# Sixteen 32x32 tiles in place of two full-width products: the weighted sums of a gathered expert layer

## The chip, the cores and the metric

The kernel runs on one core of a Trainium2 chip. The metric is the device time of one execution in microseconds. The kernel before took 2930.46 us (median of three runs, 2928.35 to 2935.43). The engines are called as in the profile: PE is TensorE, PEld its weight loads, DVE VectorE, ACT ScalarE, POOL GpSimd, SP SyncE.

## The reference

Everything is float32. The first block has two layers of attention followed by a retrieval layer (PEER), and a second block (retention, gated delta net, routed experts) follows. The change touches the retrieval alone. For each chunk of 128 tokens it is

```python
u_sel = jnp.take(u, eidx, axis=0)
a = jax.nn.gelu(jnp.einsum('chkd,cd->chk', u_sel, xc), approximate=False)
w = (g * a).astype(x.dtype)
v_sel = jnp.take(v, eidx, axis=0)
return jnp.einsum('chk,chkd->cd', w, v_sel)
```

with 8 heads h and 16 experts k for each token c, so 128 selected rows for each token, and D = 1024. There are 256 tokens, so two chunks, in each of two layers. The last line, the weighted sum of the gathered v rows, is what is changed.

## The kernel before

**The loop.** In each layer, `n` runs from 0 to 255: `c = n // 128` is the chunk, `n % 128` the selected row of each of the 128 tokens. Token p lies on partition p. For each n:

- POOL issues `gather(n)` (L2419), an indirect DMA that brings u and v of one expert for each token side by side, 128 rows of 2048 floats, into `landing(n)`, one of `GATHERS = 8` places. It first waits until the weighted sum n-8 has used the place (`("used", "gather", l, n - 8)`).
- DVE runs `dots(n)` (L1341): the dot product of the u half with the token's h.
- ACT runs `weigh(n)`: Gelu, times the softmax weight, and then `diagonals[n % 2]`, the identity scaled by the weight of each partition (L125, 128x128). It waits for the weighted sum n-2 first, since there are two diagonals.
- PE runs `weighted_sum(n)` (L155 is its helper): the diagonal is the stationary operand, the v half the moving one, two products of 512 columns into two banks of PSUM, accumulated over 128 n.

**Beside it.** Each engine carries other work in its own fixed program order between these steps: `route(q + 1)` on DVE (the top-k of the next quarter of the rows, in 24 pieces at n % 64 = 2, 4, ... 48), and a `background` generator on all engines which advances one step at the n that `beside(l, n)` names: every sixth n in layer 0, every third in layer 1 (the second block's context work). POOL advances its background five n behind its gathers, so a background step of POOL which waits for DVE holds back the gathers behind it.

**The ends of the chunks.** When the sum of a chunk is complete, `finish(c)` on DVE adds it to `ALPHA * h` from PSUM (L89, two instructions of 128x512), and a layer norm follows. `finish(0)` starts on DVE after `dots(130)` (`NORM_AT[0] = 130`), and its steps are spread over the n up to 138. `finish(1)` stands after the loop, and the next stage waits for it. Chunk 0 accumulates in banks 0 and 1, chunk 1 in banks 2 and 3 (`SUMS`); the background has banks 4 to 7 (`OTHERS`). `fresh` makes PE wait until a bank's old content was read. Vector instructions in a chain wait each for the one before.

Of the kernel before, what the change touches and what calls it, by code (L numbers as in the profile page):

```python
# [5 lines left out]
P = 128  # L6
ALU = mybir.AluOpType
# [183 lines left out]


GATHERS = 8
SUMS, OTHERS = ((0, 1), (2, 3)), (4, 5, 6, 7)
WQ_AT = (4, 8, 16, 0)
UNITS = [(0, 0), (0, 1), (1, 0), (1, 1)]
ROUTE_PIECES, EXP_AT, WEIGHTS_AT = 24, 50, 54
# [101 lines left out]
def build(nc, d, out):  # L299
    import numpy as np  # L300
    ctx = ExitStack()
    with ctx:
# [53 lines left out]
        def ar(o, n):  # L356
            assert o + n <= ARENA
            return arena[:, o:o + n]
# [30 lines left out]
        norm_scratch = ar(2048, 1024)  # L389
        SC = ar(0, 4096)  # L390
        gs, aa = ar(9056, 256), ar(9312, 256)
        diagonals = [ar(8800, 128), ar(8928, 128)]
        mod_rows = ar(20480, 2048)
        silu_cols = ar(19840, 256).rearrange("p (k s) -> p k s", k=8)

# [22 lines left out]
        def tensor_program(pe):  # L418
# [178 lines left out]
            def peer(l, background):  # L597
                qT = ar(14720, 4096).rearrange("p (m t) -> p m t", m=16)
                keys = R(12, 2)
                s = 2 * l + 1  # L600

                def turned_rows(c):
                    pe.wait_ge(*at("h", s, c))
                    for k0 in (0, 4):
                        b = fresh("hT", s, c, k0)
                        turn4(b, lambda k: h[:, c, k * P:(k + 1) * P], k0, "hT", s, c, k0)

                def queries(i, c):
                    b = fresh("q", l, i, c)
                    pe.wait_ge(*at("loaded", "wq", l, i))  # L610
                    for k0 in (0, 4):
                        pe.wait_ge(*at("out", "hT", s, c, k0))
                    for m in range(4):
                        for k in range(8):
                            t = pe.mm(b[:, m * P:(m + 1) * P], R(WQ_AT[i], 4)[:, k * 512 + m * P:k * 512 + (m + 1) * P],
                                      hT[:, k, c * P:(c + 1) * P], k == 0, k == 7)
                    pe.done(t, ("ps", "q", l, i, c))
                    if c == 1:
                        pe.tell(("used", "wq", l, i))

                def scores(c, hf):
                    for j in (2 * hf, 2 * hf + 1):
                        b = fresh("s", l, c, j)
                        pe.wait_ge(*at("loaded", "keys", l))
                        pe.wait_ge(*at("out", "q", l, j, c))
                        for m in range(4):
                            hp = 4 * j + m
                            t = pe.mm(b[:, m * P:(m + 1) * P], qT[:, hp, c * P:(c + 1) * P], keys[:, hp * P:(hp + 1) * P])
                        pe.done(t, ("ps", "s", l, c, j))
                    pe.tell(("used", "keys", l))  # L630

                def weighted_sum(n, two):

                    c, k = n // 128, n % 128
                    pe.wait_ge(*at("diagonal", l, n))
                    for x in range(2):
                        t = pe.mm(two[x][:, :], diagonals[n % 2], landing(n)[:, D + 512 * x:D + 512 * x + 512],
                                  k == 0, k == 127)
                    pe.done(t, ("used", "gather", l, n))
                    if k == 127:  # L640
                        pe.tell(("ps", "acc", l, c, 0), ("ps", "acc", l, c, 1))

                for hf in range(2):
                    for c in range(2):
                        if hf == 0 and c == 0:
                            turned_rows(0)
                        queries(2 * hf, c)
                        queries(2 * hf + 1, c)
                        if hf == 0 and c == 0:
                            turned_rows(1)  # L650
                        scores(c, hf)
                for n in range(256):
                    if n % 128 == 0:
                        two = [fresh("acc", l, n // 128, x, among=SUMS[n // 128]) for x in range(2)]
                    weighted_sum(n, two)
                    advance(background, beside(l, n))
                for _ in background:
                    pass
# [407 lines left out]
        def vector_program(v):  # L1066
# [220 lines left out]
            def peer(l, background):  # L1287
# [55 lines left out]
                        accum_out=aa[:, n:n + 1]), ("dots", l, n))  # L1343

                def finish(c):
                    for i in range(2):
                        x = h[:, c, i * 512:(i + 1) * 512]
                        v.wait_ge(*at("ps", "acc", l, c, i))
                        v.stt(x, x, ALPHA, tile_of("acc", l, c, i)[:, :], ALU.mult, ALU.add, ("out", "acc", l, c, i))
                    yield from layer_norm_parts(2 * l + 2, (c,), R(14, 1), R(15, 1), (("ln2", l, 0), ("ln2", l, 1)))  # L1350
                    yield

# [589 lines left out]
        def scalar_program(a):  # L1942
# [110 lines left out]
            def peer(l, background):  # L2053
# [21 lines left out]
                def weigh(n):  # L2075
# [5 lines left out]
                    a.act(w, w, ACT.Copy, scale=gs[:, n:n + 1])  # L2081
                    if n > 1:
                        a.wait_ge(*at("used", "gather", l, n - 2))
                    a.act(diagonals[n % 2], ident, ACT.Copy, ("diagonal", l, n), scale=w)

                for hf in range(2):
                    for c in range(2):
# [685 lines left out]
def constants():  # L2773
# [3 lines left out]
    t = {}  # L2777
# [33 lines left out]
            rows[n * x:n * x + n, j] = T * (j % 2)  # L2811
    t["slot_rows"] = rows
    t["rel"] = i[None, :] - i[:, None]
    t["fold"] = i[:, None] % 32 == np.arange(2)[None, :]
    at, o = {}, 0
    for k, v in t.items():
# [82 lines left out]
```

## Time and profile before

| | |
|---|---|
| time, median of three runs | 2930.46 us |
| time of the profiled execution | 2929.8 us |
| its span | 2928.0 us |
| granted TensorE clock over the span | 0.92 |
| gather loop of layer 0, from first to last landing | about 260 to 936 us |
| gather loop of layer 1 | about 1158 to 1830 us |
| TensorE records | 9692 weight loads, 9692 matmuls |

A float32 product stands in the trace as two weight loads and two matmul records, so a weighted sum before is four matmul records. Busy times are sums over records of an engine; the DMA share is the mean busy share of the core's 16 DMA engines.

### The profile page before, as it was taken

To read this page: it belongs to the slowest core of one execution; us is meant where nothing else is said; L and a number is where in the kernel's file an instruction comes from. 1 tells how busy PE (TensorE), PEld (TensorE's weight loads), DVE (VectorE), ACT (ScalarE), POOL (GpSimd) and SP (SyncE) were. 2 spreads that over 40 slices of the span, in tenths; PEclk is the share of its full clock that TensorE was granted. 3 is DMA by queue.
4 is the path that set the end of the run, shared out by engine and by line. 5 is a ranking of instruction groups with operands and counts; after the bars stand their busy time and mean duration, and the time that the engine had idled before them with its cause. 6 is when DMAs were issued, how large, how long until landed. Compare 5 with 4: busy or idle time off the path is not lost.

```text
span 2928.0 us, 29445 instructions
## 1 busy us (share of the span) xinstructions
PE 2373.3 (81%) x9692; PEld 1312.7 (45%) x9692; DVE 1583.3 (54%) x3250; ACT 840.9 (29%) x2292; POOL 849.7 (29%) x723
## 2 busy tenths in 40 slices
PE   6989798888887989798888998889878787667673
PEld 3657333343422559353444443568764532222221
DVE  4426857678545545888989765455552522121111
ACT  1412443434433311343443533322210111111110
POOL 1002443435432111455455553012110111222221
PEclk9999999999999889999999999899989778888887
DMA  7744999999999414999999999412112599999994
GB/s 281 278 153 191 421 422 418 416 422 389 418 423 372 169 55 162 378 421 375 410 382 406 407 422 406 158 44 73 58 62 101 213 404 401 388 390 382 382 380 142
DMA packets 130130, 891.18 MB, mean 304 GB/s; under 512 B 23216, under 2 KB 23600, under 8 KB 31792
## 3 DMA queue, kind: packets, MB, share of 16 engines
q0 software_dynamic: 86976, 553.74, 47.0%
q1 hardware_dynamic: 42992, 335.46, 28.6%
q8 instruction: 79, 1.29, 0.2%
q14 instruction: 83, 0.68, 0.1%
HBM read 880.18 MB, written 40.37 MB: 314 GB/s over the span
## 4 chain that ended last, share of the span: by engine, by line
PE 42%; DMA 26%; DVE 23%; ACT 4%; issue 3%; SPq 1%; POOL 1%; DVEq 0%; ACTq 0%; POOLq 0%
PE ps L155 40%; DMA ring<-in_peer_uv,idx_u 11%; DVE ring L1341 7%; DMA ring<-in_w_gu 6%; DVE arena L76 5%; DMA ring<-in_w_down 3%; ACT arena L125 3%; PE ps L158 2%; DMA arena<-in_peer_uv,idx_u 1%; DVE arena L109 1%; DVE iu L113 1%; DVE arena L1341 1%; SPq L2601 1%; DMA arena<-in_w_gu 1%; DMA arena<-in_w_down 1%
## 5 line engine op out<-in xcount | busy, mean ns | idle before, releaser
L155 PE MATMUL ps<-ring,arena 128*128 128x512 f32 (+3 forms) x3456 | 1292.9, 650 | 297.6 <-ACT arena L125 171.5
L155 PEld LDWEIGHTS ps<-ring,arena 128*128 128x128 f32 (+2 forms) x3456 | 476.6, 176 | 983.4 <-issue 599.0
L1341 DVE CUSTOM_DVE_ANT_0 ring<-ring,h 128x1024 f32<-128x1024 f32 x448 | 560.2, 1250 | 291.8 <-DMA ring<-in_peer_uv,idx_u 255.7
L2419 POOL DMA_INDIRECT ring<-in_peer_uv,idx_u x448 | 506.3, 1130 | 684.7 <-PE ps L155 540.9
L155 PE MATMUL ps<-arena 128*128 128x128 f32 (+7 forms) x2504 | 489.9, 377 | 92.7 <-ACT arena L125 34.3
L125 ACT ACTIVATE arena<-arena 128x1 f32<-128x1 f32 (+3 forms) x1093 | 294.2, 269 | 741.0 <-DVE arena L1341 632.8
L155 PEld LDWEIGHTS ps<-arena 128*128 128x128 f32 (+3 forms) x2504 | 309.8, 190 | 257.7 <-issue 147.7
L76 DVE TENSOR_TENSOR arena<-arena,ps 128x512 f32<-128x512 f32 (+1 forms) x158 | 93.7, 593 | 433.4 <-ACT arena L125 359.6
L125 ACT ACTIVATE arena<-ps 128x512 f32<-128x512 f32 (+5 forms) x192 | 106.4, 554 | 757.0 <-PE ps L155 708.8
L155 PE MATMUL ps<-ring,hT 128*128 128x512 f32 (+2 forms) x896 | 311.3, 509 | 15.4 <-DVE hT L97 9.9
L125 ACT ACTIVATE arena<-cst,arena 128x128 f32<-128x128 f32 x512 | 205.5, 401 | 127.4 <-PE ps L155 86.5
L155 PEld LDWEIGHTS ps<-ring,hT 128*128 128x128 f32 x896 | 174.2, 201 | 141.6 <-issue 115.9
L2556 POOL DMA_INDIRECT y_tab<-arena,iu x64 | 100.1, 1565 | 435.5 <-DVE arena L97 309.0
L134 POOL TENSOR_TENSOR small<-small,cst 128x1 f32<-128x1 f32 (+3 forms) x42 | 46.8, 1114 | 562.2 <-DVE small L84 548.1
L155 PE MATMUL ps<-hT,ring 128*128 128x128 f32 (+1 forms) x1280 | 180.5, 304 | 12.0 <-ACT hT L125 12.0
L155 PEld LDWEIGHTS ps<-hT,ring 128*128 128x128 f32 x1280 | 169.8, 198 | 20.6 <-issue 10.5
L158 PE MATMUL ps<-cst,arena 128*128 128x128 f32 (+1 forms) x706 | 115.3, 313 | 57.6 <-DVE arena L76 30.0
L158 PEld LDWEIGHTS ps<-cst,arena 128*128 128x128 f32 (+1 forms) x706 | 93.8, 158 | 114.5 <-issue 45.5
L97 DVE COPY arena<-ps 128x512 f32<-128x512 f32 (+5 forms) x102 | 59.6, 584 | 150.3 <-PE ps L155 81.7
L134 POOL TENSOR_TENSOR arena<-arena,cst 128x512 f32<-128x512 f32 (+2 forms) x52 | 68.9, 1325 | 217.2 <-DVE arena L76 118.5
L1341 DVE CUSTOM_DVE_ANT_0 arena<-arena,h 128x1024 f32<-128x1024 f32 x64 | 82.1, 1283 | 40.6 <-DMA arena<-in_peer_uv,idx_u 35.0
L2419 POOL DMA_INDIRECT arena<-in_peer_uv,idx_u x64 | 72.8, 1138 | 102.7 <-PE ps L155 100.0
(116 smaller groups left out, 1383.5 us busy)
## 6 DMA issues: line engine op xcount, KB each, us to landing
ring<-in_w_gu SPq DMA_DIRECT2D x98, 1024.0 KB, 28.8
ring<-in_w_down SPq DMA_DIRECT2D x52, 1024.0 KB, 29.4
ring<-in_w_in SPq DMA_DIRECT2D x16, 2048.0 KB, 12.4
arena<-in_w_gu SPq DMA_DIRECT2D x30, 1024.0 KB, 29.6
ring<-in_w_mod SPq DMA_DIRECT2D x12, 2048.0 KB, 8.0
ring<-in_peer_wq SPq DMA_DIRECT2D x8, 2048.0 KB, 8.3
ring<-in_w_o SPq DMA_DIRECT2D x6, 2048.0 KB, 15.2
ring<-in_w_gates SPq DMA_DIRECT2D x12, 1024.0 KB, 4.9
```

Of the source, the lines that this page charges most:

```text
L76: self.done(self.e.tensor_tensor(o, a, b, op), *names)
L97: self.done(self.e.tensor_copy(o, a), *names)
L109: self.done(self.e.max(out=o, in_=a), *names)
L113: self.done(self.e.max_index(o, m, a), *names)
L125: self.done(self.e.activation(o, a, f, **k), *names)
L134: self.done(self.e.tensor_tensor(o, a, b, op), *names)
L155: return self.e.matmul(o, lhsT, rhs, start=start, stop=stop, skip_group_check=True)
L158: return self.e.transpose(o, src, ident)
L1341: v.done(v.e.tensor_tensor_reduce(out=row, in0=row, in1=h[:, n // 128, :], scale=1.0, scalar=0.0, op0=ALU.mult, op1=ALU.add, accum_out=aa[ ...
L2419: g.e.indirect_dma_start(out=landing(n), out_offset=None, in_=d["peer_uv"], in_offset=bass.IndirectOffsetOnAxis(ap=idx_u[:, n:n + 1], axis ...
L2556: g.e.indirect_dma_start(out=y_tab, out_offset=index(m.add_to, n), in_=m.yb[s % 2], in_offset=None, bounds_check=2 * T - 1, oob_is_err=Fal ...
L2601: sp.e.dma_start(o, src).then_inc(sem, 16)
```

## The change

Each weighted sum is done as sixteen products instead of two. D is cut in four quarters x of 256 columns. For each quarter, the 128 tokens are cut in four groups r of 32, and group r of quarter x is computed on its own 32x32 tile of the array: rows 32r to 32r+31, columns of group r XOR x. So quarter x has its own bank, and in it the token groups stand permuted by r XOR x. The stationary operand is a 32-column diagonal (`ident4` repeats a 32x32 identity for each group of 32 partitions). All four banks 0 to 3 are used by both chunks. `finish` now reads quarter 0 in one instruction and the others in four each, which undo the permutation.

```diff
-SUMS, OTHERS = ((0, 1), (2, 3)), (4, 5, 6, 7)
+SUMS, OTHERS = (0, 1, 2, 3), (4, 5, 6, 7)
...
-        diagonals = [ar(8800, 128), ar(8928, 128)]
+        diagonals = [ar(8800, 32), ar(8928, 32)]
...
-                    for x in range(2):
-                        t = pe.mm(two[x][:, :], diagonals[n % 2], landing(n)[:, D + 512 * x:D + 512 * x + 512],
-                                  k == 0, k == 127)
+                    for x in range(4):
+                        for r in range(4):
+                            i, o = slice(32 * r, 32 * r + 32), slice(32 * (r ^ x), 32 * (r ^ x) + 32)
+                            t = pe.mm(four[x][o, 0:256], diagonals[n % 2][i, :], landing(n)[i, D + 256 * x:D + 256 * x + 256],
+                                      k == 0, k == 127)
...
-                        two = [fresh("acc", l, n // 128, x, among=SUMS[n // 128]) for x in range(2)]
-                    weighted_sum(n, two)
+                        four = [fresh("acc", l, n // 128, x, among=SUMS) for x in range(4)]
+                    weighted_sum(n, four)
...
-                    for i in range(2):
-                        x = h[:, c, i * 512:(i + 1) * 512]
-                        v.wait_ge(*at("ps", "acc", l, c, i))
-                        v.stt(x, x, ALPHA, tile_of("acc", l, c, i)[:, :], ALU.mult, ALU.add, ("out", "acc", l, c, i))
+                    v.wait_ge(*at("ps", "acc", l, c, 0))
+                    for q in range(4):
+                        for r in range(1 if q == 0 else 4):
+                            i, o = (slice(0, P),) * 2 if q == 0 else (slice(32 * r, 32 * r + 32),
+                                                                      slice(32 * (r ^ q), 32 * (r ^ q) + 32))
+                            x = h[i, c, 256 * q:256 * q + 256]
+                            v.stt(x, x, ALPHA, tile_of("acc", l, c, q)[o, 0:256], ALU.mult, ALU.add,
+                                  ("out", "acc", l, c, q))
...
-                    a.act(diagonals[n % 2], ident, ACT.Copy, ("diagonal", l, n), scale=w)
+                    a.act(diagonals[n % 2], C("ident4"), ACT.Copy, ("diagonal", l, n), scale=w)
...
+    t["ident4"] = i[:, None] % 32 == np.arange(32)[None, :]
```

## Rows read from the trace of the kernel before

**Rows 1.** The page: busy times of the engines, and GB/s in 40 slices.

```profile
PE 2373.3 (81%) x9692; PEld 1312.7 (45%) x9692; DVE 1583.3 (54%) x3250; ACT 840.9 (29%) x2292; POOL 849.7 (29%) x723
...
GB/s 281 278 153 191 421 422 418 416 422 389 418 423 372 169 55 162 378 421 375 410 382 406 407 422 406 158 44 73 58 62 101 213 404 401 388 390 382 382 380 142
```

**Rows 2.** Busy time by stretch: window, length, engines, granted clock, DMA share, GB/s.

```profile
278.00:936.00 658.00, 547.48 (x1269) 231.18 (x1267) 439.88 (x906) 260.29 (x803) 276.26 (x251) 0.96 1.00 415
640.00:665.00 25.00, 18.07 (x37) 7.29 (x37) 22.71 (x58) 9.31 (x31) 11.59 (x9) 0.93 0.97 388
1172.00:1829.60 657.60, 567.00 (x1802) 278.67 (x1801) 526.53 (x1013) 273.99 (x835) 325.94 (x272) 0.97 0.98 401
1190.00:1215.00 25.00, 18.34 (x45) 8.62 (x46) 21.88 (x62) 11.58 (x31) 5.74 (x6) 0.80 0.99 411
1215.00:1240.00 25.00, 20.32 (x66) 9.74 (x64) 22.95 (x49) 8.27 (x27) 14.31 (x13) 1.00 0.80 304
1370.00:1395.00 25.00, 19.61 (x67) 9.85 (x66) 22.99 (x47) 7.78 (x25) 16.13 (x12) 1.00 0.83 328
1525.00:1550.00 25.00, 19.69 (x63) 9.84 (x64) 22.77 (x61) 8.45 (x28) 16.01 (x13) 0.93 0.83 330
1700.00:1800.00 100.00, 89.73 (x291) 43.32 (x290) 64.44 (x98) 38.95 (x125) 47.78 (x43) 1.00 1.01 421
```

**Rows 3.** The longest wait of DVE from 1190 to 1284 us: total, times, longest.

```profile
DVE ring L1341 <- DMA ring<-in_peer_uv,idx_u: 0.6, 1, 0.6
```

**Rows 4.** Timeline of POOL: start, length, instruction, idle before it, releaser.

```profile
1217.68 0.94 POOL L2419 DMA_INDIRECT ring<-in_peer_uv,idx_u  x1 [0.44 <-PE ps L155]
1223.05 3.46 POOL L134 TENSOR_TENSOR arena<-arena,cst 128x512 f32<-128x512 f32 x2 [4.43 <-DVE arena L76]
1226.66 0.96 POOL L2419 DMA_INDIRECT ring<-in_peer_uv,idx_u  x1
...
1511.00 0.94 POOL L2419 DMA_INDIRECT ring<-in_peer_uv,idx_u  x1 [7.21 <-PE ps L155]
```

**Rows 5.** Timeline of the end of layer 1's gather loop, all engines.

```profile
1827.19 1.23 DVE L1341 CUSTOM_DVE_ANT_0 ring<-ring,h 128x1024 f32<-128x1024 f32 x1 [1.26 <-DMA ring<-in_peer_uv,idx_u]
...
1829.65 1.23 DVE L1341 CUSTOM_DVE_ANT_0 ring<-ring,h 128x1024 f32<-128x1024 f32 x1 [1.22 <-DMA ring<-in_peer_uv,idx_u]
...
1831.54 0.40 ACT L125 ACTIVATE arena<-cst,arena 128x128 f32<-128x128 f32 x1
1831.99 0.30 PEld L155 LDWEIGHTS ps<-ring,arena 128*128 128x128 f32 x2 [1.30 <-ACT arena L125]
1831.99 1.98 PE L155 MATMUL ps<-ring,arena 128*128 128x512 f32 x4 [0.47 <-ACT arena L125]
...
1834.02 1.41 DVE L89 SCALAR_TENSOR_TENSOR h<-h,ps 128x512 f32<-128x512 f32 x2 [3.13 <-PE ps L155]
```

**Rows 6.** Timeline of DVE: finish(0) of layer 1, and eight chained instructions of 256 columns.

```profile
1508.33 1.41 DVE L89 SCALAR_TENSOR_TENSOR h<-h,ps 128x512 f32<-128x512 f32 x2
```

```profile
23.60 3.65 DVE L89 SCALAR_TENSOR_TENSOR arena<-cst 128x256 f32<-128x256 f32 x8
```

**Rows 7.** Timeline of PE: four column tiles of 32, 512 columns moving.

```profile
125.44 1.92 PE L155 MATMUL ps<-ring,arena 128*32 128x512 f32 x16
```

**Rows 8.** Timeline of PE and of its weight loads: a burst on column tiles of 32.

```profile
2358.38 1.10 PE L155 MATMUL ps<-arena 128*32 128x2 f32 x64 [2.87 <-DVE arena L76]
```

```profile
2358.38 1.01 PEld L155 LDWEIGHTS ps<-arena 128*32 128x32 f32 x64 [3.77 <-DVE arena L76]
```

**Rows 9.** Timeline of PE: an unbroken stream of full-width loads and matmuls.

```profile
1132.80 14.46 PE L155 MATMUL ps<-hT,ring 128*128 128x128 f32 x128
```

**Rows 10.** The page: instruction DMA queue, packets, MB, share of 16 engines.

```profile
q8 instruction: 79, 1.29, 0.2%
```

More of the change, by code:

```diff
@@ L630, in scores, with weighted_sum @@
                     pe.tell(("used", "keys", l))
-                def weighted_sum(n, two):
+                def weighted_sum(n, four):
                     c, k = n // 128, n % 128
                     pe.wait_ge(*at("diagonal", l, n))
-                    for x in range(2):
-                        t = pe.mm(two[x][:, :], diagonals[n % 2], landing(n)[:, D + 512 * x:D + 512 * x + 512],
-                                  k == 0, k == 127)
+                    for x in range(4):
[3 more added lines that the diff above has]
+                                      k == 0, k == 127)
                     pe.done(t, ("used", "gather", l, n))
                     if k == 127:
-                        pe.tell(("ps", "acc", l, c, 0), ("ps", "acc", l, c, 1))
+                        pe.tell(*(("ps", "acc", l, c, x) for x in range(4)))
                 for hf in range(2):
```

## The prediction

> **What bounds the kernel now.** I read the page first. It names PE as the busiest engine, 81% of the span, and shows DMA at about 421 GB/s in a long early and a long middle stretch [rows 1]. These are the two gather loops, and together they are 1.35 ms of 2.93. So the first question is whether PE or DMA sets their pace. The timeline at the end of layer 1 answers it for a quiet stretch: two dots start 2.46 us apart, each after a wait for its landing, and the sum's four matmul records take 1.98 us [rows 5]. A gather is 1 MB (128 rows of 8 KB), and at 421 GB/s that is 2.49 us. So one n costs DMA 2.49 us and PE 1.98 us and the share of the background. DMA sets the pace there; PE, at 90% busy, runs close behind [rows 2].
>
> The windows tell where DMA falls short of 421 GB/s, and this is all that a faster PE could win inside the loops. Layer 0 moved 415 GB/s over 658 us: 658 x 6/421 = 9 us lost. Layer 1 moved 401 over 657.6 us: 657.6 x 20/421 = 31 us lost [rows 2]. Together 40 us.
>
> Then I looked for what holds the gathers back in layer 1. Three windows of 25 us have 304, 328 and 330 GB/s, and lose 6.9, 5.5 and 5.4 us, 18 of the 31 [rows 2]. The timeline of POOL shows the reason for the first: after the gather at 1217.68, POOL waits 4.43 us for DVE, runs two background instructions of 3.46 us together, and only then issues the next gather at 1226.66 [rows 4]. Which engine is DVE waiting for in turn? For none: from 1190 to 1284 us its longest wait is 0.6 us [rows 3], and its busy time is 22 to 23 of 25 us [rows 2], the rest being the short gaps between chained instructions. So where layer 1 loses most, DVE is the bound, through its route pieces and background, and POOL's place behind it turns this into late gathers. PE is busy 18 to 20 of 25 us there and does not decide.
>
> **The change part by part.** I make the sum against the profiled execution (2929.8 us; the median of the runs is 0.7 us higher).
>
> *The sum itself on PE.* Two products of 512 columns become sixteen of 256 on tiles of 32x32. The trace has no tile that is cut in rows as well. The nearest row is four column tiles side by side: 16 records of 512 columns in 1.92 us, 0.12 us for each, while full-width records of the same length take about 0.5 us (1.98 for four) [rows 5, 7]. So four column tiles run at once. If row groups run at once as well, 32 records of 256 columns need a quarter of 1.71, so 0.43 us. The other limit is how fast PE gets its instructions: 32 loads and 32 matmuls for each n. A burst of 64 loads and 64 matmuls on 32-column tiles took 1.10 us, 8.6 ns for each record [rows 8], so 64 records take 0.55 us. The slowest feed I can find in an unbroken stream is 128 loads and 128 matmuls in 14.46 us, 56 ns for each record [rows 9], which is array time and an upper bound. I take the burst, whose shape is nearer: 0.55 us and a start of some 0.2, 0.75 us for a single sum. With PE less busy its granted clock may well fall from the 0.96 of these loops towards half (the window with PE busy 18 of 25 us already shows 0.80 [rows 2]), so between 0.75 and 1.2 us; I take 1.0 us against 1.98.
>
> The Trainium skill has a rule against such small products: in "TensorE: Matmul & The Clock Gate", section "Wait — 56ns, not 53.3ns?", the sequencer needs about 62 ns for each matmul when hardware decode is off. By it, as an estimate, 32 matmuls would need 1.98 us, and the change would win nothing on PE. The burst of 64 in 1.10 us speaks against it.
>
> *Term A, the ends of the two loops.* After the last landing the path is dots, weight, diagonal, sum, finish(1) [rows 5]. The sum gives back 1.98 - 1.0 = 1.0 us, and the diagonal of 32 columns instead of 128 (0.40 us before) about 0.1. finish(1) goes from two instructions in 1.41 us to thirteen of 256 columns. DVE's chained pitch for 256 columns is 3.65/8 = 0.456 us [rows 6], whatever the number of partitions that I assume; thirteen take 5.93 us, so 4.5 us more. Net 3.4 us for each layer: +6.8. Bounds 5 and 8.
>
> *Term B, finish(0) in the middle.* The same 4.5 us come to DVE after dots(130). In layer 1 it stands at 1508, DVE is as full behind it as in the stretch of [rows 3] (22.77 of 25 us), and a POOL block like that of [rows 4] follows in the 330 GB/s window [rows 2]. So all of it arrives at the gathers: +4.5. In layer 0 finish(0) stands near 610, and the window from 640 to 665 has DVE busy 22.71 of 25 us at 388 GB/s [rows 2]; it is the one short window there, DVE is freer around it, and a part falls in gaps: I take +2, between 0 and 4.5. Together +6.5, bounds 0 and 9. Since both chunks now share the banks, PE's sum 128 waits for finish(0), and behind it wait PE's later sums and background, ACT's diagonal 130, and gather 136 on POOL. In layer 1, finish(0) would end at 1508.33 + 5.93 = 1514.3, and gather 136 was issued at 1511.00 [rows 4, 6]; so it slips by some 4 to 5 us. Seven gathers of 2.49 us, 17 us of DMA work, are outstanding then and cover it. I put nothing for this wait.
>
> *Term C, instructions.* For each n PE gets 64 records instead of 8: 512 x 56 = 28,672 more. The instruction queue q8 moved 1.29 MB in 79 packets, and 1.29 MB over PE's 19,384 records is 67 bytes for each, so I read q8 as PE's queue, with 256 records in a packet of 16 KB [rows 1, 10]. That makes 1.9 MB or 117 packets more, through the same 16 engines that bound the loops. 0.2% of 16 x 2928 us is 94 us of engine time, 1.19 us for each packet. Spread evenly, 117 x 1.19/16 = 8.7 us, and in about four fifths of the loops' time DMA is the bound: +7. If they never met a saturated engine it is 0; if the worst engine gets twice the mean, 17; if all fell to one engine, 139. "Runtime: NRT & Kernel Launch" of the Trainium skill, section "Instruction fetch mechanics", says that instructions come in blocks of 16 KiB or 256 and that the fetch is hidden. The block size agrees with [rows 10]. By that rule term C is 0 and the forecast about 2940.
>
> *Term D, places free earlier.* The sum releases its place about 1 us earlier, and PE's queue of sums behind background steps gets shorter. Of the 40 us of lost DMA time, 18 stand behind POOL's waits for DVE and stay. Of the other 22 many are gathers limited by DVE in the same saturated stretches, so I take 4 us, a microsecond for each of a few late gathers: -4, bounds 0 and -22.
>
> Sum: 2929.8 + 6.8 + 6.5 + 7 - 4 = 2946.1 us, with the 0.7 us to the median 2947. The bounds give 2929.8 + 5 - 22 = 2913 and 2929.8 + 8 + 9 + 17 = 2964, without the single-engine case. The new constant adds 32 columns to a load at the start, and I cost it at nothing.
>
> **The rivals.**
> - *The release of places decides after all.* POOL's gathers often wait for PE: 7.21 us before the one at 1511.00 [rows 4]. If a faster PE removed all 40 us and the slack swallowed finish(0), the time would be 2930 - 40 + 6.8 + 7 = 2904. It decides if gathers come early enough that POOL's blocks no longer empty the queue. Against it: DVE has no waits there [rows 3]. 0.08.
> - *Same.* finish(0) falls in gaps and the packets are hidden: 2930.5 + 6.8 - 4 = 2933. 0.20.
> - *Row groups do not run at once.* Then four columns at a time as in [rows 7], about 1.7 us and the start as before; gains of A and D vanish: 2947 + 2 + 4 = 2953. 0.08. By the Trainium skill's rule on the sequencer, as an estimate, it would come to about the same.
> - *PE starves for instructions.* At 56 ns a record one n takes 3.6 us, 1.1 more than DMA's 2.49, over 512 n +570: about 3520. It decides from 39 ns a record (2.49/64). 0.04.
> - *Instruction packets pile up on one engine*: 132 us over the forecast, 3079. 0.04.
> - The forecast itself: 0.56, its own range 2936 to 2960.
>
> **How the numbers follow.** I take 0.3%, 9 us, as what a measurement can tell from no change. Faster (under 2922): the first rival and a little of term D, 0.10. Same: the second rival and the low edge of the forecast, 0.25. Slower: 0.65. The range reaches from the second rival with its spread, 2929, to the third with its own, 2968. It leaves out the first, fourth and fifth, 0.16.
>
> **What would show it.** On the page: about 57,000 to 58,000 instructions, q8 near 196 packets, PE's busy share well down and its granted clock in the loops below 0.96. In the timeline at the end of the loops: 32 matmul records of 32x256 within 0.5 to 1.2 us, and finish as thirteen instructions over 5.9 us. In layer 1's windows: DVE as busy as before, DMA still short by POOL's wait for DVE, and the third block 4 to 5 us later within the loop than before. In quiet windows such as 1700 to 1800 us: slightly under 421 GB/s. The prediction is wrong if the windows of 304 to 330 GB/s fill up (then D was the main term), if quiet windows lose more than 1.5% (then C), or if dots come further apart than 2.5 us in quiet stretches with PE as releaser.

## The result, and the profile after

The changed kernel takes 2953.24 us (median of four runs, 2951.98 to 2956.14), the kernel before 2930.26 beside it: ratio 1.0083, 95% interval 1.0069 to 1.0096. It is 23 us slower, where 17 slower was forecast. The profiled execution has a span of 2952.0 us against 2928.0.

The page of the changed kernel, to be read beside [rows 1, 10]:

```profile
span 2952.0 us, 58166 instructions
...
PE 2043.1 (69%) x24028; PEld 1172.3 (40%) x24028; DVE 1595.3 (54%) x3294; ACT 799.6 (27%) x2292; POOL 848.5 (29%) x723
...
PEclk9888577565755889686767775799998788888787
...
q8 instruction: 190, 3.11, 0.4%
```

PE has 14,336 more loads and as many more matmuls, and is 330 us less busy. Its granted clock is down to 0.5 to 0.8 in the loops, and queue q8 moves 111 packets of 16 KB more.

The windows of the changed kernel, beside [rows 2]; the window from 1240 to 1265 us is new, because the first block has moved there:

```profile
278.00:936.00 658.00, 372.85 (x8196) 141.37 (x8188) 438.67 (x908) 236.65 (x789) 276.46 (x253) 0.61 1.00 413
...
1172.00:1829.60 657.60, 414.18 (x8748) 237.69 (x8746) 522.48 (x1022) 252.88 (x824) 329.03 (x275) 0.72 0.98 401
1215.00:1240.00 25.00, 12.17 (x298) 5.16 (x296) 22.61 (x53) 11.33 (x32) 8.09 (x8) 0.70 0.96 398
1240.00:1265.00 25.00, 14.71 (x292) 8.47 (x292) 22.85 (x59) 8.00 (x29) 13.94 (x12) 0.70 0.85 339
1370.00:1395.00 25.00, 11.51 (x252) 5.11 (x268) 22.85 (x55) 10.55 (x33) 8.88 (x7) 0.51 0.75 304
1525.00:1550.00 25.00, 11.01 (x236) 5.38 (x236) 22.83 (x50) 5.01 (x16) 8.73 (x8) 0.57 0.68 259
1700.00:1800.00 100.00, 68.91 (x1443) 42.22 (x1440) 61.98 (x95) 35.73 (x125) 49.22 (x45) 0.76 1.01 419
```

PE's busy time in layer 1 fell from 567 to 414 us, and the same window still moves 401 GB/s. The three short windows are still there (339, 304, 259), with DVE at 22.8 of 25 us in each, while PE is busy half of the time. In the quiet window the rate is 419 instead of 421.

The end of layer 1's loop in the changed kernel, beside [rows 5], and finish(0) of both layers on DVE, beside [rows 6]:

```profile
1848.38 1.23 DVE L1343 CUSTOM_DVE_ANT_0 ring<-ring,h 128x1024 f32<-128x1024 f32 x1 [1.22 <-DMA ring<-in_peer_uv,idx_u]
...
1850.85 1.23 DVE L1343 CUSTOM_DVE_ANT_0 ring<-ring,h 128x1024 f32<-128x1024 f32 x1 [1.24 <-DMA ring<-in_peer_uv,idx_u]
...
1852.74 0.32 ACT L125 ACTIVATE arena<-cst,arena 128x32 f32<-128x32 f32 x1
1853.12 0.29 PEld L155 LDWEIGHTS ps<-ring,arena 32*32 32x32 f32 x32 [2.18 <-ACT arena L125]
1853.12 1.17 PE L155 MATMUL ps<-ring,arena 32*32 32x256 f32 x32 [1.30 <-ACT arena L125]
1854.46 5.84 DVE L89 SCALAR_TENSOR_TENSOR h<-h,ps 128x256 f32<-128x256 f32 x13 [2.37 <-PE ps L155]
```

```profile
617.61 5.84 DVE L89 SCALAR_TENSOR_TENSOR h<-h,ps 128x256 f32<-128x256 f32 x13
...
1525.29 5.84 DVE L89 SCALAR_TENSOR_TENSOR h<-h,ps 128x256 f32<-128x256 f32 x13
```

The dots still come 2.47 us apart, each after its landing. The sum takes 1.17 us instead of 1.98, and finish 5.84 us instead of 1.41.

The start times of the dots, n = 0, 128, 136 and 255 of each layer, divide every trace in the same way. The table has one profiled execution of each kernel; the last three rows are of the experiments with chunk 0's norm moved to n = 200. All in us.

| kernel | before loop 0 | loop 0 | in it n 128 to 136 | between | loop 1 | in it n 128 to 136 | rest | span |
|---|---|---|---|---|---|---|---|---|
| before | 260.3 | 676.1 | 22.4 | 221.3 | 671.9 | 27.6 | 1098.3 | 2928.0 |
| changed | 265.1 | 685.4 | 26.8 | 223.4 | 676.9 | 31.7 | 1101.1 | 2952.0 |
| e1_finish13 | 265.5 | 680.8 | 26.8 | 225.6 | 673.5 | 31.7 | 1102.2 | 2947.6 |
| e2_unpermuted | 262.1 | 682.1 | 22.4 | 220.9 | 674.0 | 27.8 | 1099.0 | 2938.2 |
| e3_zeros14 | 266.5 | 810.8 | 33.5 | 227.6 | 833.7 | 27.1 | 1106.3 | 3244.9 |
| e4_tiles64 | 262.7 | 674.9 | 23.1 | 219.1 | 666.9 | 27.9 | 1097.6 | 2921.2 |
| e5_before_lag8 | 260.5 | 680.4 | 22.4 | 218.3 | 666.7 | 26.7 | 1095.5 | 2921.4 |
| e6_before_lag3 | 265.3 | 687.0 | 22.4 | 223.1 | 685.5 | 27.6 | 1098.4 | 2959.3 |
| e7_tiles64_lag8 | 258.5 | 673.0 | 23.1 | 217.9 | 669.9 | 27.0 | 1095.3 | 2914.6 |
| e8_after_lag8 | 265.4 | 681.1 | 26.8 | 223.9 | 676.8 | 30.8 | 1100.7 | 2947.9 |
| e12_sp_waits | 258.2 | 676.5 | 22.4 | 221.1 | 691.6 | 27.6 | 1636.6 | 3483.9 |
| e9_before_norm200 | 260.6 | 674.5 | 19.9 | 220.4 | 664.4 | 23.3 | 1101.7 | 2921.6 |
| e10_finish13_norm200 | 258.3 | 674.9 | 19.9 | 224.2 | 662.0 | 23.3 | 1103.7 | 2923.0 |
| e11_tiles64_norm200 | 264.8 | 673.4 | 20.7 | 218.1 | 660.8 | 23.5 | 1100.9 | 2917.9 |

The changed kernel's 24.0 us of span are 4.8 before the first loop, 9.3 and 5.0 in the loops (4.4 and 4.1 of these between n = 128 and 136), 2.1 between the layers and 2.8 after. Single traces differ in code that no version changes: the first column reaches from 258.2 to 266.5, and the profiled execution of a kernel lies up to 10 us from the kernel's median (e6 2961.15 against 2951.32, e7 2916.41 against 2924.88). So a difference of one column between two traces is certain only to several us. The column n 128 to 136 is firmer: in layer 0 it is 22.4 in all five traces that have the old finish at n = 130 and PE's full-width or (r, r) sums, and 26.8 in all three with thirteen instructions there; in layer 1 it is 26.7 to 27.8 and 30.8 to 31.7.

### The profile page after: what moved, and what is told of

Same layout as the page of the kernel before. It is cut to its first block, busy times and chain, and to the rows that moved or that the text cites. A ratio compares the mean times of both kernels' runs of the same rounds, so it can differ in the third digit from the quotient of the medians.

```text
span 2952.0 us, 58166 instructions
## 1 busy us (share of the span) xinstructions
PE 2043.1 (69%) x24028; PEld 1172.3 (40%) x24028; DVE 1595.3 (54%) x3294; ACT 799.6 (27%) x2292; POOL 848.5 (29%) x723
## 4 chain that ended last, share of the span: by engine, by line
PE 36%; DMA 31%; DVE 24%; issue 3%; ACT 3%; SPq 1%; POOL 1%; DVEq 0%; another core or an unknown queue 0%; ACTq 0%; POOLq 0%
PE ps L155 34%; DMA ring<-in_peer_uv,idx_u 18%; DVE ring L1343 8%; DMA ring<-in_w_gu 7%; DVE arena L76 5%; DMA ring<-in_w_down 3%; ACT arena L125 2%; PE ps L158 2%; DVE arena L109 1%; DVE iu L113 1%; DVE arena L1343 1%; SPq L2607 1%; DMA arena<-in_w_gu 1%; DVE h L89 1%; DVE arena L97 1%
## 5 line engine op out<-in xcount | busy, mean ns | idle before, releaser
L155 PE MATMUL ps<-ring,arena 32*32 32x256 f32 (+4 forms) x16000 | 926.4, 556 | 580.5 <-ACT arena L125 431.4
L155 PEld LDWEIGHTS ps<-ring,arena 32*32 32x32 f32 (+3 forms) x16000 | 302.0, 127 | 1087.9 <-ACT arena L125 685.6
L155 PE MATMUL ps<-arena 32*32 32x256 f32 (+8 forms) x4296 | 490.6, 456 | 152.2 <-ACT arena L125 82.3
L155 PEld LDWEIGHTS ps<-arena 32*32 32x32 f32 (+4 forms) x4296 | 327.9, 174 | 299.7 <-ACT arena L125 136.7
L125 ACT ACTIVATE arena<-cst,arena 128x32 f32<-128x32 f32 x512 | 164.5, 321 | 112.1 <-PE ps L155 59.8
```

The costliest lines, as they stand in the source:

```text
L125: self.done(self.e.activation(o, a, f, **k), *names)
L155: return self.e.matmul(o, lhsT, rhs, start=start, stop=stop, skip_group_check=True)
```

## The experiments

The kernel before took 2927.36 us beside e1 to e4 (17 runs), 2927.88 beside e5 to e8 (23) and 2927.71 beside e9 to e12 (21). Ratios are to these.

### e1_finish13: only the thirteen instructions of finish

```diff
-                    for i in range(2):
-                        x = h[:, c, i * 512:(i + 1) * 512]
-                        v.wait_ge(*at("ps", "acc", l, c, i))
-                        v.stt(x, x, ALPHA, tile_of("acc", l, c, i)[:, :], ALU.mult, ALU.add, ("out", "acc", l, c, i))
+                    v.wait_ge(*at("ps", "acc", l, c, 0))
+                    for q in range(4):
+                        for r in range(1 if q == 0 else 4):
+                            i = slice(0, P) if q == 0 else slice(32 * r, 32 * r + 32)
+                            x = h[i, c, 256 * q:256 * q + 256]
+                            v.stt(x, x, ALPHA, tile_of("acc", l, c, q // 2)[i, 256 * (q % 2):256 * (q % 2) + 256],
+                                  ALU.mult, ALU.add, ("out", "acc", l, c, q // 2))
```

> The kernel before, with only finish changed: thirteen chained instructions of 256 columns (three quarters of D in groups of 32 partitions) in place of two of 512. The sums are as before. My theory (terms A and B): 4.5 us more at both ends and at finish(0) of layer 1, 2 to 4.5 us at finish(0) of layer 0, so +15 to +18, about 2947 us. Rival, finish(0) is absorbed in DVE's gaps: only the two ends count, +9, 2939 us. If the time stays within 3 us of before, the finish is not what made the changed kernel slower.

2947.73 us (2939.43 to 2953.5), ratio 1.0066, interval 1.0047 to 1.0084: 20 us slower, most of what the change costs. Two of its six executions took 2939 us and four 2947 to 2954. The timeline of this kernel shows the four finishes as in the changed one; here is DVE at the end of layer 1:

```profile
1849.79 5.83 DVE L89 SCALAR_TENSOR_TENSOR h<-h,ps 128x256 f32<-128x256 f32 x13 [3.13 <-PE ps L155]
```

The parts stand where terms A and B put them: 4.4 and 4.1 us between n = 128 and 136 of the two layers, 4.3 between the layers and 3.9 after. Layer 0's is as large as layer 1's. Together they are 16.7 us, of the 15 to 18 that I expected; in this trace the first loop also starts 5.2 us later. The steps are not made up for later: against before, this kernel's dots are 0.1 us early at n = 128 of layer 0, 4.4 late at 132 and 4.7 at 255; in layer 1 they are 2.6 early, then 1.6 late at 132 and still 1.6 at 255. (That layer 1's whole loop is only 1.6 us longer comes from its first eight n, which took 2.0 us less.) And since this kernel has the old banks, and the changed kernel has the same two steps of 4.4 and 4.1, the sharing of the banks adds nothing to them. Behind n = 136 no run has the shared banks alone: in layer 0 the changed kernel loses another 1.2 us to n = 144, where e1 gains 1.2.

### e2_unpermuted: only the small tiles and their instructions

Sixteen products for each row as in the change, but group r always on tile (r, r), two quarters in the two halves of one bank, and finish as before. What it changes in the computation: a tile starts its sum in both halves of a bank, and the sums that come out are not quite the reference's; the instructions and their sizes are those of the change.

```diff
+                    for x in range(4):
+                        for r in range(4):
+                            i, y = slice(32 * r, 32 * r + 32), slice(256 * (x % 2), 256 * (x % 2) + 256)
+                            t = pe.mm(two[x // 2][i, y], diagonals[n % 2][i, :],
+                                      landing(n)[i, D + 256 * x:D + 256 * x + 256], k == 0, k == 127)
```

> Sixteen 32x32 products for each row as in the changed kernel, but every token group stays on its own columns (tile r, r for all quarters), so two banks for each chunk, finish and the banks' waits are as before. It has the changed kernel's instruction count without its finish. Only four of the sixteen tiles are ever in use, so the sum should take about 1.7 to 2.0 us, as before. Theory (term C): instruction packets on the DMA engines cost +5 to +9 us, 2936 to 2939 us, and quiet windows move 418 to 419 GB/s instead of 421. Rival, packets are hidden: 2930 us plus or minus 2. Rival, products on one tile do not overlap at all: 16 x 0.43 us for each row, over 4000 us.

2939.44 us (2934.33 to 2940.77), ratio 1.0041, interval 1.0028 to 1.0055. The last sum, the quiet window and the page's row of q8 of this kernel:

```profile
1841.37 1.93 PE L155 MATMUL ps<-ring,arena 32*32 32x256 f32 x32 [1.44 <-ACT arena L125]
```

```profile
1700.00:1800.00 100.00, 92.22 (x1416) 53.62 (x1408) 65.97 (x97) 34.91 (x122) 51.64 (x43) 1.00 1.01 420
```

```profile
q8 instruction: 191, 3.13, 0.4%
```

And the windows around the last sum, of the changed kernel and then of e2, for their granted clock:

```profile
1850.00:1855.00 5.00, 2.34 (x64) 0.58 (x64) 1.74 (x4) 1.32 (x5) 0.00 (x0) 0.50 0.00 2
```

```profile
1838.00:1844.00 6.00, 3.85 (x64) 1.80 (x64) 1.87 (x3) 0.82 (x3) 0.00 (x0) 1.00 0.00 0
```

Two things follow. First, 32 records on four tiles take 1.93 us at the full clock, about the 1.98 of four full-width records; on sixteen tiles the same 32 take 1.17 us at half of it (0.50, the 1.2 GHz level). Each tile works through its own records one after another (eight here, two in the change), and the start times in the traces show it: here the 32 matmul records start in eight groups of four, with about 196 ns between the groups, in the change in two groups of sixteen, with 315 ns between them. So the gain comes from all sixteen tiles being in use, which is what the permutation is for. Second, with the sum as slow as before and finish unchanged, what is left is the 112 packets and PE's 64 records for each n in place of 8: the two loops are 6.0 and 2.1 us longer, 8 together, and the timed difference is 12 us (8 to 16). Term C said 7. This run does not tell the packets from PE's work on the records; PE's busy time in the quiet window is 92.2 of 100 us instead of 89.7.

### e3_zeros14: 28 more small record pairs between the full-width ones

Fourteen products of zero (an off-diagonal 32x32 block of the diagonal, two columns) between the two full-width products of each row, added to the sum.

```diff
+                        if x:
+                            for z in range(14 if 0 < k < 127 else 0):
+                                pe.mm(two[0][32:64, 2 * z:2 * z + 2], diagonals[n % 2][0:32, 32:64],
+                                      landing(n)[0:32, D:D + 2], False, False)
```

> The kernel before with fourteen extra products of 32x32 by 2 columns for each row between its two full products (their stationary operand is the zero corner of the diagonal, so the result is unchanged): 56 more PE records for each row, as many as the changed kernel has, and nothing else. Theory (term C): +5 to +9 us from the packets, and up to 0.5 us for each row more on PE, which DMA covers in quiet stretches: 2935 to 2942 us. Rival, packets cost nothing: 2930 us. If PE's longer sum itself mattered, windows with PE as releaser of gathers would grow and the time go past 2945.

3249.21 us (3242.97 to 3250.82), ratio 1.1099, interval 1.1082 to 1.1117. The windows of layer 1 and two of its loads in the timeline of this kernel:

```profile
1172.00:1829.60 657.60, 634.28 (x6254) 418.86 (x6255) 420.23 (x931) 200.85 (x581) 221.67 (x188) 0.97 0.75 278
1700.00:1800.00 100.00, 97.34 (x1001) 58.44 (x999) 76.82 (x176) 35.00 (x106) 42.58 (x36) 0.98 0.86 316
```

```profile
1747.88 1.27 PEld L155 LDWEIGHTS ps<-ring,arena 32*32 32x32 f32 x30 [0.76 <-issue]
...
1750.77 1.27 PEld L155 LDWEIGHTS ps<-ring,arena 32*32 32x32 f32 x30 [0.76 <-issue]
```

I meant this run to add packets at no cost on PE, and it does not: 28 tiny loads on one tile, with two of the full-width ones, take 1.27 us, with a stop of 0.76 us ahead of them; the 28 start 32 ns apart. A sum with its share then takes 2.89 us (1750.77 - 1747.88), over DMA's 2.49, and PE is the bound, busy 97% of the quiet window at 316 GB/s. It says nothing on term C. What it does show is that the rival in which PE starves is real as a mechanism: 2.89 us for 64 records is 45 ns each, over the 39 from which that rival decides. It took tiny pairs on one tile beside a full-width sum; the changed kernel's 64 records in 1.17 us, spread over tiles, are 18 ns each.

### e4_tiles64: four tiles of 64x64

Four products of 512 columns on tiles of 64x64, two banks for a chunk as before, finish in three instructions.

```diff
+                        for r in range(2):
+                            i, o = slice(64 * r, 64 * r + 64), slice(64 * (r ^ x), 64 * (r ^ x) + 64)
+                            t = pe.mm(two[x][o, :], diagonals[n % 2][i, :], landing(n)[i, D + 512 * x:D + 512 * x + 512],
+                                      k == 0, k == 127)
```

> Four products on 64x64 tiles of 512 columns for each row (two halves of D, the second with the two token groups swapped), two banks for each chunk as before, finish in three instructions of 512 columns. 16 PE records for each row instead of 64, finish 0.7 us longer than before instead of 4.5. Theory: sum of about 1.0 to 1.2 us, term A about 0, term B +1, term C +1, term D -2 to -4: 2927 to 2931 us, no difference from before. Rival, a faster PE frees places and pays once its side costs are gone: 2905 to 2920 us.

2924.52 us (2918.53 to 2928.16), ratio 0.9991, interval 0.9982 to 0.9999. The last sum of its layer 0, the end of its layer 1, and its q8:

```profile
939.88 1.99 PE L155 MATMUL ps<-ring,arena 64*64 64x512 f32 x8 [0.47 <-ACT arena L125]
...
1825.91 1.09 PE L155 MATMUL ps<-ring,arena 64*64 64x512 f32 x8 [0.84 <-ACT arena L125]
1827.07 2.13 DVE L89 SCALAR_TENSOR_TENSOR h<-h,ps 128x512 f32<-128x512 f32 x3 [2.21 <-PE ps L155]
```

```profile
q8 instruction: 95, 1.56, 0.2%
```

The same idea with a quarter of the instructions has a sum of 1.09 us where the granted clock is full (1.00 from 1825.9 to 1827.0) and of 1.99 us where it is at half (0.50 from 939.9 to 941.8), which is no less than before's 1.98. It has 16 packets more, and 0.7 us more for a finish. Its loops are 1.2 and 5.0 us shorter in the traces. So the faster sum is worth at most some 6 us in the loops (term D: 4, of bounds 0 and 22), and the timed medians, 2.8 us apart in all, say rather less; it is real and small.

### e5, e6, e8 and e7: POOL's background further behind its gathers, or nearer

```diff
-                for n in range(256 + 5):
+                for n in range(256 + 8):
...
-                    if n >= 5:
-                        advance(background, beside(l, n - 5))
+                    if n >= 8:
+                        advance(background, beside(l, n - 8))
```

e6 has 3 in place of 8; e7 has this edit on e4, e8 on the changed kernel.

> Edit: the kernel before, with POOL's background eight n behind its gathers instead of five, so that a background step that waits for DVE stands behind three more gathers; all else unchanged. Theory (of the 31 us of DMA time that layer 1 loses, 18 are lost because POOL waits for DVE in three background blocks while its gathers stand behind it): three more gathers of 2.49 us are then queued ahead of each block, the windows of 304 to 330 GB/s rise towards 400, and the time falls by 5 to 12 us, ratio 0.996 to 0.998. Rival (DVE itself is full in these stretches, so the dots come no earlier whatever POOL does, or the eight places are used up anyway): the place is given free by a sum that stands behind the same dots, and nothing moves, within 2 us.

> Edit: the kernel before, with POOL's background three n behind its gathers instead of five. Theory (POOL's wait for DVE costs DMA time): the blocks hold back the gathers two n longer, layer 1's three short windows become shorter still, and the time rises by 3 to 15 us. Rival (DVE's fullness alone sets the loss): within 2 us.

> Edit: four products for each row on tiles of 64x64 (e4_tiles64: 2924.5 us, 0.9991 of before) and POOL's background eight n behind its gathers. Theory (a faster sum can give only what POOL's blocks leave it): the two gains add or more, 2912 to 2918 us, ratio 0.994 to 0.997. Rival (both touch the same lost DMA time, or none): no more than the better of the two alone, 2920 to 2925 us.

> Edit: the changed kernel, with POOL's background eight n behind its gathers instead of five. Theory (the faster sum of the changed kernel, which gave back only about 2 to 3 us, is kept from more by POOL's blocks): 5 to 15 us less than the changed kernel, 2938 to 2948 us. Rival (the places are held by dots and not by the sum): as the changed kernel, 2951 to 2955 us.

e5: 2930.1 us (2923.21 to 2939.36), ratio 1.0008, interval 0.9998 to 1.0018. e6: 2951.32 (2951.01 to 2961.15), 1.0086, 1.0071 to 1.01. e7: 2924.88 (2916.41 to 2932.8), 0.9994, 0.9985 to 1.0003. e8: 2943.5 (2942.31 to 2950.33), 1.0057, 1.0043 to 1.0071.

My theory for e5 fell. The first of layer 1's blocks, two windows of the kernel before, then the same two of e5:

```profile
1215.00:1240.00 25.00, 20.32 (x66) 9.74 (x64) 22.95 (x49) 8.27 (x27) 14.31 (x13) 1.00 0.80 304
1240.00:1265.00 25.00, 20.99 (x70) 10.80 (x71) 22.84 (x41) 9.70 (x31) 12.18 (x11) 1.00 1.01 422
```

```profile
1215.00:1240.00 25.00, 21.04 (x67) 10.00 (x65) 22.99 (x49) 7.78 (x25) 12.89 (x12) 0.98 0.96 353
1240.00:1265.00 25.00, 20.70 (x70) 10.62 (x71) 22.76 (x41) 10.20 (x32) 14.29 (x12) 1.00 0.97 373
```

This block is smoothed out and nothing is won: 304 + 422 and 353 + 373 are both 726. DVE has 23 of 25 us in all four rows, so the hole in the transfers is here only where DVE's lack of time shows. The other two blocks are less even: the second gains (328 + 423 before, 389 + 403 in e5, from 1370 to 1420 us, again with DVE near 23 of 25), the third does not (330 + 420, then 352 + 385). The trace of e5 has layer 1's loop 5.2 us shorter and layer 0's 4.3 us longer, and the median does not fall. So between 5 and 8 POOL's distance decides nothing in sum; that DVE alone decides in every block is not shown. Nearer is another matter. In e6 POOL's steps really hold the gathers back: both loops are longer, by 11 and 14 us. For the changed kernel a distance of 8 gave a ratio of 1.0057 instead of 1.0083, some 8 us (the intervals overlap at their ends). But e8's five executions fall in two groups, 2942 to 2944 and 2950 us, about as far apart as the first column's 258 and 266. The traced one is of the upper group and starts its first loop at 265.4, like the changed kernel's; against that one it gains 4 us, in layer 0's loop. More than these 4 is not shown, nor why they are won there. e7 adds nothing to e4, as e5 added nothing to before.

### e9, e10, e11: chunk 0's norm where DVE is free

```diff
-NORM_AT = (130, 131, 133, 137, 138)
+NORM_AT = (200, 201, 203, 207, 208)
```

e9 has it on the kernel before, e10 on e1, e11 on e4. From n = 192 on no route piece is left.

> Edit: the kernel before, with finish(0) and the rest of chunk 0's norm spread over n = 200 to 208 instead of 130 to 138, where no route piece stands beside them (about 6.5 us of DVE work in each layer). Theory (DVE's full stretches, not POOL's place nor PE, set the lost DMA time, and what is taken off DVE there comes back whole): layer 1's loop is 5 to 7 us shorter, layer 0's 2 to 6, the time 2917 to 2923 us. Rival (the loss has another cause, and DVE's work moves freely): within 3 us of before.

> Edit: e1 (finish in thirteen instructions, 2947.7 us) with chunk 0's norm at n = 200 to 208. Theory (term B was 4.5 us in each layer because DVE was full behind n = 130): both finish(0) are covered at n = 200, the step between n = 128 and 136 disappears and no other takes its place; against e9 only the two finish(1) remain, +9 us, 2926 to 2932 us, some 15 to 20 below e1. Rival (4.5 us on DVE's chain cost 4.5 us wherever they stand): e9 + 18 us, and a step of 4 us at n = 200 instead.

> Edit: e4 (four products on tiles of 64x64, 2924.5 us, 0.9991) with chunk 0's norm at n = 200 to 208. Theory: the two gains add, 2912 to 2920 us, the best of all. Rival (same lost DMA time, won once): as e9.

e9: 2917.11 us (2915.46 to 2923.42), ratio 0.9964, interval 0.9951 to 0.9978. e10: 2929.46 (2924.83 to 2940.25), 1.0012, 1.0001 to 1.0023. e11: 2919.84 (2917.6 to 2920.66), 0.9972, 0.9963 to 0.9982.

The windows of e9 around n = 128, beside the 330 GB/s of [rows 2]:

```profile
1500.00:1525.00 25.00, 17.87 (x43) 8.13 (x44) 22.10 (x55) 11.27 (x35) 11.69 (x9) 0.86 0.97 393
1525.00:1550.00 25.00, 22.66 (x81) 11.89 (x80) 22.56 (x60) 9.28 (x29) 16.71 (x13) 1.00 1.01 412
```

This settles what bounds the stretch behind n = 128. With some 6.5 us of DVE work taken away, the step from n = 128 to 136 is 4.3 us shorter in layer 1 and 2.5 in layer 0, the hole is filled, and layer 1's loop is 7.5 us shorter. It is 10.6 us for one line, and the lowest median of all. The edit moves POOL's step of the norm along with DVE's, so the two are not told apart here; and for the blocks at 1215 and 1370 us, where no run moved work, that DVE is the bound rests on the windows. e10 shows the same for the thirteen instructions: at n = 200 the loops are no longer than e9's (+0.4 and -2.4), so 4.4 us more on DVE cost nothing where DVE has room, and only the two finish(1) are left (3.8 between the layers and 2.0 after in the traces; 12 us in the timed medians, 9 by the rows of finish). e11 is e9 again: the gain of the small tiles, 3 us in e4, is not added. For the changed kernel I did not try it; there finish(0) cannot move to n = 200, since PE's sum 128 waits for it to empty the shared banks.

### e12_sp_waits: packets for an engine that has nothing to do

```diff
+            for n in range(255):
+                for _ in range(112):
+                    sp.e.wait_ge(*at("dots", 1, n))
```

> Edit: the kernel before, with 112 waits on an already reached semaphore for each n of layer 1 in SP's program (28,560 instructions of SP, which has nothing else to do then), so that instruction packets are fetched in layer 1's loop and no other engine gets any work. Theory (term C: the packets take time on the saturated DMA engines, 1.19/16 us each): about 110 packets more, if SP's instructions are 64 bytes too, and layer 1's loop 5 to 9 us longer. Rival (the fetch is hidden, and the 8 us in the loops of e2_unpermuted come from PE's 64 records for each n): layer 1's loop within 3 us of before's 671.9. If SP needs over 22 ns for a wait, it falls behind the loop and the loads of the next stage come late; then only the loop is read.

3486.33 us (3484.99 to 3497.58), ratio 1.1921, interval 1.19 to 1.1942. SP falls far behind and the loads of the next stage come late (the 1636.6 in the table), so only the loop can be read. From the page:

```profile
q8 instruction: 78, 1.28, 0.1%
q14 instruction: 194, 1.59, 0.1%
```

SP's packets are in q14 (111 more, of 8 KB). SP reached its waits only at about n = 130, and from there to the end 43 packets more than before fell in the loop, which is 19.7 us longer. Dots of this kernel in the quiet stretch:

```profile
1785.13 1.23 DVE L1341 CUSTOM_DVE_ANT_0 ring<-ring,h 128x1024 f32<-128x1024 f32 x1 [2.12 <-DMA ring<-in_peer_uv,idx_u]
...
1787.49 1.23 DVE L1341 CUSTOM_DVE_ANT_0 ring<-ring,h 128x1024 f32<-128x1024 f32 x1 [0.30 <-DMA ring<-in_peer_uv,idx_u]
...
1789.97 1.23 DVE L1341 CUSTOM_DVE_ANT_0 ring<-ring,h 128x1024 f32<-128x1024 f32 x1 [1.25 <-DMA ring<-in_peer_uv,idx_u]
...
1793.21 1.22 DVE L1341 CUSTOM_DVE_ANT_0 ring<-ring,h 128x1024 f32<-128x1024 f32 x1 [2.00 <-DMA ring<-in_peer_uv,idx_u]
```

About every third interval is 3.1 to 3.4 us instead of 2.48, and a packet of q14 starts every 8 us: about one late landing for each. From n = 212 to 254 that is 9.1 us for 14 packets, 0.65 us each. In the changed kernel the same stretch has 9 packets of q8 more and is 0.9 us longer, 0.1 us each, although one lasts 1.07 us and one of SP's 0.32. (e1, with no packet more, is 0.9 us shorter there, so the 0.1 is hardly above the noise; the 0.65 is.) So the fetch is not hidden here, which speaks against the rival. But the price is not the packet's time over sixteen engines either. That SP's packets all meet one of the sixteen, on which each gather then waits, while PE's are spread, would explain the two prices; the traces don't name the engine, and SP's own waits may disturb something too, so that the packets cause the 19.7 us is likely and not shown. That stays open.

## Why the prediction was right, point by point

**What bounds.** Right in both loops. DMA sets the pace where it is quiet, and PE can give up 150 us of its time in layer 1 for nothing. That DVE is the bound in the blocks was an argument then; e9 and e10 show it for the one behind n = 128. One step of the argument was too strong: moving POOL's place from 5 to 8 behind its gathers wins nothing in sum for the kernel before (e5; 726 and 726 in the first block), so at its distance of 5 that place is no loss by itself.

**The sum on PE.** I took 1.0 us within 0.75 to 1.2, and it took 1.17, with the granted clock at half as feared. The 32 records stand in the trace at 37 ns each. By the Trainium skill ("TensorE: Matmul & The Clock Gate", section "Wait — 56ns, not 53.3ns?") the sequencer's 62 ns for each matmul, which holds with hardware decode off, would have made it 1.98, as an estimate; the trace does not agree.

**Term A, +6.8.** This term was right. In layer 1 the path from the start of the last dots to the end of finish went from 5.78 us (1829.65 to 1835.43 in [rows 5]) to 9.45 (1850.85 to 1860.30 above), and in layer 0 from 5.77 to 9.45: 3.7 us each where I had 3.4, 7.3 together. In e1, with finish alone, it is 10.20, so 4.4 each; the difference is what the shorter sum and diagonal give back. Thirteen instructions took 5.84 us, against 5.93 worked out from eight. The columns between and after the loops grew by only 2.1 and 2.8 in the changed kernel; the other -2.4 us of them lie in code that is not changed.

**Term B, +6.5.** It measured 8.5 (4.4 and 4.1), at the upper bound of 9. The part that was mis-sized is layer 0's, for which I took 2: I let some of it fall in gaps, because only one window there falls to 388 GB/s. But from 613 to 638 us of the kernel before, behind its finish(0), DVE is busy 21.7 of 25 us, and this is all that it waited for from 610 to 665 us, no landing among it:

```profile
DVE arena L82 <- ACT arena L125: 1.2, 1, 1.2
```

So DVE had no gap there in which 4.4 us could go unseen, although the transfers ran at 422 GB/s meanwhile. That the wait of sum 128 for the banks costs nothing is right as far as n = 136: e1 has the same steps without that wait, though in the changed kernel the wait is plain to see in POOL's timeline:

```profile
1520.02 0.94 POOL L2425 DMA_INDIRECT ring<-in_peer_uv,idx_u  x1 [0.75 <-PE ps L155]
1532.96 1.04 POOL L2425 DMA_INDIRECT ring<-in_peer_uv,idx_u  x1 [12.01 <-PE ps L155]
```

**Term C, +7.** Rows of before gave the packets' time on the DMA engines, but none what it does to the gathers; e2 has the term at 8 by the loops and at 12 (8 to 16) by the times, PE's work on the records included. q8 got 111 packets more where I worked out 117. From first to last dots of the two loops 136 packets fall instead of 25, 1.07 us each, and the gather's packet behind one takes 0.80 instead of 0.31 us: 111 x 1.56/16 = 10.8 us, as an estimate, if spread evenly. The Trainium skill ("Runtime: NRT & Kernel Launch", section "Instruction fetch mechanics") has the fetch hidden, by which C would be 0. On the DMA engines it is not hidden here, as the 0.80 us show, and e2 is 12 us above before, so the measurement decides for these loops. How much of the 12 is the fetch, and how its price forms, is open (e12).

**Term D, -4.** The changed kernel's loops grew by 14.3 us; less term B (8.5) and e2's 8.1 that leaves -2.3. In e4, with few packets, the loops are 6.2 us shorter. Each is a difference of single traces, so that the term is small is shown, and its size is not; that there is a gain at all rests on e4's times (0.9991, with the interval just under 1). The first rival, the release of places decides, needed -40 and is refuted by e4 and e11.

**What the sum did not hold.** 4.8 us before the first loop, where no instruction is changed. The granted clock differs there: from 100 to 150 us it is 0.80 instead of 0.86, and the same matmuls take longer. PE before, then in the changed kernel:

```profile
109.04 1.92 PE L155 MATMUL ps<-ring,arena 128*32 128x512 f32 x16
```

```profile
108.90 3.04 PE L155 MATMUL ps<-ring,arena 128*32 128x512 f32 x16
```

The first loop starts between 258 and 266 us over all the traces, on either side in kernels with the same code there (e5 260.5, e6 265.3). The clock of that window goes with it: 0.80 in all eight traces that start the loop at 262.1 or later, e1 and e6 among them, which have no small tiles at all, and 0.93 in the five others beside before's 0.86. So the 4.8 us are the luck of the execution and no cost that the change is shown to have. Of the 24.0 us of span 21.6 belong to terms A to D, where the sum had 16.3 (A 0.5 more, B 2.0 more, C and D together 2.8 more); 4.8 belong to that clock, and -2.4 to unchanged code behind the loops. The forecast was near because the mechanisms were right, and what it missed is too little for layer 0's finish, and for the instructions and the faster sum together. Whether the clock falls early in every run of the changed kernel its times don't say; e8, the other trace with these tiles, starts its first loop at 265.4 too.

## What to carry to other kernels

Before speeding up an engine, ask in each stretch which one is full, and look for it in small windows. Here it was DMA in the quiet ones and DVE in the one where its work was moved, and 330 us less on PE bought some 2 us in the loops, e4's 239 us less at most 6. What the speed-up charges to the full engines is what counts: eleven small instructions more at each finish on DVE, and 28,672 records whose fetch shares the DMA engines with the gathers. Work on a full engine that may be done later is worth moving first, as one line with 10.6 us shows.

## What the runs showed of the hardware that I had not expected

- The tiles of the array each work off their own records: 32 records of 32x256 took 1.93 us on four tiles at the full clock and 1.17 us on sixteen at half. Four tiles of 64x64 at half the clock took 1.99 us, no less than the full-width products at the full clock, 1.98 (e4).
- Tiny matmuls on one tile between full-width ones are dear: 32 ns from start to start and a stop of 0.76 us (e3), where the burst of before, on four column tiles, had 64 pairs in 1.10 us.
- A gather's packet right behind an instruction packet takes 0.80 us instead of 0.31. In e12's quiet stretch each 8 KB packet of an idle engine's instructions went with 0.65 us more of the loop.
- A granted clock of half did not slow the gathers: from 900 to 936 us of the changed kernel it is 0.50 and the rate 420 GB/s, with PE busy 17.1 of 36 us. It shows in the 1.17 us of the sum at the two ends.
